# Two pads in SBUF that move every large tile to a multiple of 512 bytes, in a float32 decoder layer on one core

## The chip, the core and the metric

The kernel runs on one NeuronCore of a Trainium2 chip. Its engines are TensorE (PE, with its weight loads shown apart as PEld), VectorE (DVE), ScalarE (ACT), GpSimd (POOL) and SyncE (SP, which here only issues DMAs). The metric is the device time of one execution in microseconds, from outside the program; lower is better.

## What is computed

One layer of a decoder over 1024 positions of width 1024, all in float32. Cut to what matters:

```python
u = rms_norm(h, g_mix);  z = u @ w_in                    # 1024 x 4512 (MLA latents, retention q/k/v/gate, two gates)
q = rms_norm(c_q) @ w_uq;  kv = rms_norm(c_kv) @ w_ukv   # MLA, 8 heads, causal softmax
y_a = causal_block_attention(q_full, k_full, v_a) @ w_proj_mla
y_r = (silu(rg) * head_group_norm(retention_chunkwise(rq, rk, rv))) @ w_proj_ret
h = h + (sigmoid(g_a) * y_a + sigmoid(g_r) * y_r) @ w_out
h = h + cross_attention(rms_norm(h) @ w_xq, rms_norm(mem) @ w_xkv) @ w_xo      # 256 memory rows
up = causal_dwconv(rms_norm(h) @ w_up)                   # 1024 x 5632, three taps
h = h + (silu(up[..., :2816]) * up[..., 2816:]) @ w_down
return rms_norm(h, g_final)
```

## The kernel before

Each float32 product is made of three: both operands are split into a high half, rounded to the type that TensorE multiplies quickly (float32r), and a low half, the difference. `mm3` (line 304) issues them: high weights by high activations (L307), high by low (L312), low weights by high (L313). Every one loads its own 128 x 128 weights and streams up to 512 columns.

The host lays all dense weights out as 168 slabs of 128 x 1024 in the order of use. SP loads a slab of 512 KB into one of the two buffers of `raw`; POOL writes its high half to `wh` (L289) and its low half to `wl` (L291), each with four slots; PE works a slab off in `dense` (line 320): two halves of 512 positions, for each half eight blocks k (or four to six), for each k one `mm3`. The slab's block k is at `wh[:, j, k*128:...]`, so 512 bytes after the one before. The first matmul of a slab that is done frees the slot before it (`w_used`), and POOL goes on. The moving operands are the layer's activations, positions along the columns: `uh`, `ul` (normed input), `yth`, `ytl` (retention's output), `oth`, `otl` (MLA's), `mih`, `mil` (the gated mix), `g0h` to `g1l` (normed for the cross-attention), `xqh`, `xql`, `f0h` to `f1l` (normed for the FFN) and `fah`, `fal` (the FFN's hidden channels, in groups of 6, 6, 6 and 4 blocks).

Not all weights that PE loads are slabs. In the MLA stage `m_pv` (L586) multiplies with the value rows `vrh`, `vrl` as weights, and the probabilities `p1h`, `p1l` (or `p0h`, `p0l`) stream; in the attention over memory the scores have `xqh`, `xql` as weights and `mkh`, `mkl` moving with 256 columns, the values `mvh`, `mvl` as weights and `xph`, `xpl` moving with 512. For the keys and values of the memory (`mth`, `mtl`, 256 columns) the weights are slabs again, and for the MLA queries (384 columns) the slabs `wh`, `wl` move and `cqh`, `cql` are the weights. Transposes go through PE too, with the identity in `cn`.

SBUF is allocated by hand. Long-lived tensors come first, one after the other, through `sb`; all large tiles come from `place(kb, ...)`, which puts tensors `kb` KB above the end of those, over one another in time:

```python
with ExitStack() as st:
    if kb:
        st.enter_context(nc.sbuf_tensor(f"below_{specs[0][0]}", [P, int(kb * 256)], f32))
    return [st.enter_context(nc.sbuf_tensor(n, s, f32r if r else f32)) for n, s, r in specs]
```

Nearly all sizes are multiples of 512 bytes, so the start of the first tensor of `sb`, and of the first of `place`, within 512 bytes is that of all that follow. Before, `raw` starts at byte 16,512 of a partition, `wh` at 24,704 and `wl` at 41,088, ending at 57,472 (128 within 512 bytes for each); the tiles start at 62,784 (320 within 512): `uh`, `hT`, `xqh`, `f1h` and `vrh` there, `f0h`, `xs` and `mih` at 128,320, `fah` at 161,088, `p1h` at 193,856. The identity in `cn` starts at 64 within 512.

Of the kernel before, what the change touches and what calls it, by code (L numbers as in the profile page):

```python
# [26 lines left out]
P = 128  # L27
# [73 lines left out]
def build(nc, x, mem, pos, slabs, small, const, out):  # L101
# [23 lines left out]
    with ctx:  # L125
        def sb(name, shape, dt=f32):
            return ctx.enter_context(nc.sbuf_tensor(name, shape, dt))
# [2 lines left out]
            return ctx.enter_context(nc.semaphore(name))  # L130


        raw = sb("raw", [P, RAWS, 1024])
        wh = sb("wh", [P, SLOTS, 1024], f32r)
        wl = sb("wl", [P, SLOTS, 1024], f32r)
# [9 lines left out]
        rsm = sb("rsm", [P, NT, 2])  # L145
        mst = sb("mst", [P, 3, MB])
        amax, aneg, asum, ainv = (sb(n, [P, 2, CH]) for n in ("amax", "aneg", "asum", "ainv"))
        ps = ctx.enter_context(nc.psum_tensor("ps", [P, 8, H2], f32))


# [1742 lines left out]
```

## Time and profile before

| | |
|---|---|
| timed runs | 2094.06, 2099.07, 2099.65 us; median 2099.07 |
| the profiled execution, first to last instruction | 2093.5 us |
| PE busy | 1955.6 us, 9308 matmuls |
| DVE, ACT, POOL busy | 909.7, 557.9, 850.0 us |
| mean granted clock of TensorE | 0.978 |

The profile shows one execution; of its own time it tells the span alone, which the three timed runs exceed by 0.6, 5.6 and 6.2 us. Busy times say how much of the span an engine works; a group of instructions tells a line, an engine, the tensors written and read, and the shape. A matmul's duration there is from its start to its modelled end, and matmuls overlap. The pace at which PE goes is read from the starts in the timeline: the distance between two rows, divided by the number of matmuls from the one to the other.

### The profile page before, as it was taken

The page shows a single profiled execution, that of the slowest core. Times are in us where ns is not written, and L with a number is a line of the kernel's source. Part 1 is how long each engine was busy: PE and PEld are TensorE (multiplying, and loading weights), DVE is VectorE, ACT ScalarE, POOL GpSimd, SP SyncE. Part 2 cuts the span into 40 slices and gives each one's busy share as a digit, 9 for nine tenths or more (in the row PEclk, how much of TensorE's full clock was granted, in tenths as well). Part 3 has the DMA queues.
Part 4 walks back from the last instruction along what each step waited for, and adds up shares of the span by engine and source line. Part 5 has one row for each costly group of instructions (what it writes and reads, how often), then busy time and mean ns, then how long its engine had stood idle before and what let it go on. Part 6 is the DMA issues. An engine that isn't in the chain of part 4 may idle for free.

```text
span 2093.5 us, 25536 instructions
## 1 busy us (share of the span) xinstructions
PE 1955.6 (93%) x9308; PEld 1595.0 (76%) x9308; DVE 909.7 (43%) x1522; ACT 557.9 (27%) x988; POOL 850.0 (41%) x324
## 2 busy tenths in 40 slices
PE   5999999999978887899998899999999999999987
PEld 4888888888767776677778878787888788878865
DVE  5454540000266665543421633665155415542564
ACT  5222231001245555212223411322022102210223
POOL 5333224565310001244327034445645555455460
PEclk9999999999989999999999999999999999999998
DMA  4101112233100003432114112111111121111111
GB/s 149 41 31 30 40 49 83 89 101 94 41 27 1 1 1 107 159 118 99 42 41 137 35 61 80 41 50 50 61 50 40 54 67 40 50 50 61 50 50 81
DMA packets 35339, 128.39 MB, mean 61 GB/s; under 512 B 4032, under 2 KB 4160, under 8 KB 35264
## 3 DMA queue, kind: packets, MB, share of 16 engines
q1 hardware_dynamic: 25776, 92.72, 14.4%
q10 hardware_dynamic: 9488, 34.61, 4.4%
q8 instruction: 54, 0.88, 0.2%
q14 instruction: 21, 0.17, 0.0%
HBM read 110.54 MB, written 16.78 MB: 61 GB/s over the span
## 4 chain that ended last, share of the span: by engine, by line
PE 76%; DVE 9%; issue 6%; ACT 5%; DMA 2%; POOL 1%; SPq 0%; ACTq 0%; DVEq 0%; POOLq 0%
PE ps L307 23%; PE ps L312 23%; PE ps L313 23%; PE ps L586 3%; POOL wl L282 1%; ACT prow L1014 1%; PE ps L565 1%; ACT pr L1175 1%; DVE p1l L1266 1%; DVE t L1269 1%; DMA xs<-in_x 1%; DVE ul L1269 1%; DVE yb L1773 0%; DVE amax L1539 0%; PE ps L737 0%
## 5 line engine op out<-in xcount | busy, mean ns | idle before, releaser
L289 POOL TENSOR_SCALAR wh<-raw 128x1024 fp32r<-128x1024 f32 x152 | 427.1, 2810 | 1129.5 <-PE ps L307 934.0
L291 POOL TENSOR_TENSOR wl<-raw,wh 128x1024 fp32r<-128x1024 f32 x152 | 384.7, 2531 | 12.7
L307 PE MATMUL ps<-uh,wh 128*128 128x512 f32 (+1 forms) x576 | 230.6, 400 | 2.4 <-DVE ul L1269 2.4
L312 PE MATMUL ps<-ul,wh 128*128 128x512 f32 (+1 forms) x576 | 227.9, 396 | 0.0
L313 PE MATMUL ps<-uh,wl 128*128 128x512 f32 (+1 forms) x576 | 227.9, 396 | 0.0
L307 PE MATMUL ps<-fah,wh 128*128 128x512 f32 x352 | 140.6, 399 | 11.4 <-DVE hF L1611 6.3
L307 PE MATMUL ps<-f0h,wh 128*128 128x512 f32 x352 | 138.9, 395 | 1.3 <-DVE z L1757 1.3
L307 PE MATMUL ps<-f1h,wh 128*128 128x512 f32 x352 | 139.0, 395 | 0.1
L313 PE MATMUL ps<-f1h,wl 128*128 128x512 f32 x352 | 138.8, 394 | 0.0
L312 PE MATMUL ps<-f1l,wh 128*128 128x512 f32 x352 | 138.8, 394 | 0.0
L313 PE MATMUL ps<-f0h,wl 128*128 128x512 f32 x352 | 138.8, 394 | 0.0
L312 PE MATMUL ps<-f0l,wh 128*128 128x512 f32 x352 | 138.8, 394 | 0.0
L313 PE MATMUL ps<-fah,wl 128*128 128x512 f32 x352 | 138.8, 394 | 0.0
L312 PE MATMUL ps<-fal,wh 128*128 128x512 f32 x352 | 138.7, 394 | 0.0
L307 PEld LDWEIGHTS ps<-uh,wh 128*128 128x128 f32 (+1 forms) x576 | 107.5, 187 | 28.4 <-DVE ul L1269 2.6
L313 PEld LDWEIGHTS ps<-uh,wl 128*128 128x128 f32 (+1 forms) x576 | 107.2, 186 | 27.6
L312 PEld LDWEIGHTS ps<-ul,wh 128*128 128x128 f32 (+1 forms) x576 | 107.3, 186 | 25.9
L1221 ACT ACTIVATE ya<-z,sm 128x512 f32<-128x512 f32 x44 | 35.9, 817 | 300.5 <-DVE z L1757 300.5
L1757 DVE TENSOR_TENSOR z<-ps,rbF 128x512 f32<-128x512 f32 x88 | 60.8, 691 | 106.5 <-PE ps L313 103.2
L1791 DVE TENSOR_TENSOR hF<-ps,hF 128x512 f32 x48 | 33.2, 691 | 149.6 <-PE ps L313 149.4
L307 PEld LDWEIGHTS ps<-fah,wh 128*128 128x128 f32 x352 | 65.8, 187 | 34.4 <-issue 9.7
L1269 DVE SCALAR_TENSOR_TENSOR ya<-z,sm,ya 128x512 f32<-128x512 f32 x88 | 67.9, 771 | 53.2 <-ACT ya L1221 49.3
(347 smaller groups left out, 4082.1 us busy)
## 6 DMA issues: line engine op xcount, KB each, us to landing
raw<-in_slabs SPq DMA_DIRECT2D x168, 512.0 KB, 3.6
xs<-in_x SPq DMA_DIRECT2D x8, 512.0 KB, 7.6
s_ga<-sig ACTq DMA_DIRECT2D x8, 512.0 KB, 2.6
s_mr<-mxr ACTq DMA_DIRECT2D x8, 512.0 KB, 4.7
xtile<-in_x ACTq DMA_DIRECT2D x8, 512.0 KB, 6.5
sab<-s_ga ACTq DMA_DIRECT2D x8, 512.0 KB, 4.1
mrb<-s_mr ACTq DMA_DIRECT2D x8, 512.0 KB, 5.1
s_h<-hT ACTq DMA_DIRECT2D x8, 512.0 KB, 2.7
```

Of the source, the lines that this page charges most:

```text
L282: pool.tensor_tensor(wl[:, j, :], raw[:, j % RAWS, :], wh[:, j, :].bitcast(f32), ALU.subtract).then_inc(S["w_ready"], 1)
L289: pool.tensor_scalar(wh[:, j, :], raw[:, j % RAWS, :], 1.0, None, ALU.mult).then_inc(S["w_hi"], 1)
L291: pool.tensor_tensor(wl[:, j, :], raw[:, j % RAWS, :], wh[:, j, :].bitcast(f32), ALU.subtract).then_inc(S["w_ready"], 1)
L307: l = pe.matmul(o, lh, rh, start=start, stop=False)
L312: pe.matmul(o, lh, rl, start=False, stop=False)
L313: return pe.matmul(o, ll, rh, start=False, stop=stop)
L565: l = pe.transpose(ps[:, 6 + q % 2, (c % CH) * P:(c % CH + 1) * P], prow[:, w % 2, c * P:(c + 1) * P], ident)
L586: return pe.matmul(ps[:, 1, qs], vv[:, c, v], pp[:, c, qs], start=start, stop=stop, skip_group_check=True)
L1221: act.activation(y[:, half(b)], z[:, 2 + b * H2:2 + (b + 1) * H2], ACT.Identity, scale=smc("cw2", c + FB * x_), bias=smc("b_conv", c + FB ...
L1269: return dve.scalar_tensor_tensor(out=o, in0=a, scalar=s_, in1=b_, op0=op0, op1=op1)
L1757: dve.tensor_tensor(z[:, 2 + b * H2:2 + (b + 1) * H2], ps[:, b, :], rbF[:, b, :], ALU.mult).then_inc(d_free[b], 1)
L1791: dve.tensor_tensor(hb, ps[:, b, :], hb, ALU.add).then_inc(d_free[b], 1)
```

## The change

Two tensors that nothing reads or writes are allocated: one of 96 float32 (384 bytes per partition) ahead of `raw`, one of 80 (320 bytes) behind the small tensors, ahead of what `place` gives out.

```diff
+        sb("line_up_slabs", [P, 96])
         raw = sb("raw", [P, RAWS, 1024])
         wh = sb("wh", [P, SLOTS, 1024], f32r)
         wl = sb("wl", [P, SLOTS, 1024], f32r)
...
         amax, aneg, asum, ainv = (sb(n, [P, 2, CH]) for n in ("amax", "aneg", "asum", "ainv"))
+        sb("line_up_tiles", [P, 80])
         ps = ctx.enter_context(nc.psum_tensor("ps", [P, 8, H2], f32))
```

The instructions of every engine, their order and their waits are the same ones. Only addresses differ:

| tensors | start within 512 bytes before | after |
|---|---|---|
| `raw`, `wh`, `wl`, `sm` | 128 | 0 |
| `cn` (identity, constants) | 64 | 448 |
| `ones_r`, `ident_r`, `mask_r` | 480 | 352 |
| all first tensors of `place` and what lies behind them in whole 512 bytes (`uh` ... `fal`, `z`) | 320 | 0 |
| `ya`, `yb` (behind `z`, which has 1026 columns) | 352 | 32 |
| `t3`, `t4` | 480 | 160 |
| `zkr`, `krow`, `kr1`, `kr2` | 384 | 64 |

Slabs move up by 384 bytes and tiles by 704. The distance from a slab's start to a tile's, within 512 bytes, is 192 before and 0 after; between two tiles, or two slabs, it is 0 in both.

## Rows read from the trace of the kernel before

**Rows 1.** The page's busy times, and the core's mean granted clock.
```profile
PE 1955.6 (93%) x9308; PEld 1595.0 (76%) x9308; DVE 909.7 (43%) x1522; ACT 557.9 (27%) x988; POOL 850.0 (41%) x324
...
core 0: 2093.5 us, clock 0.978
```

**Rows 2.** The chain that ended last: shares of the span by engine.
```profile
PE 76%; DVE 9%; issue 6%; ACT 5%; DMA 2%; POOL 1%; SPq 0%; ACTq 0%; DVEq 0%; POOLq 0%
```

**Rows 3.** Groups of lines (busy us, mean ns, idle before and its releaser), POOL's split.
```profile
L289 POOL TENSOR_SCALAR wh<-raw 128x1024 fp32r<-128x1024 f32 x152 | 427.1, 2810 | 1129.5 <-PE ps L307 934.0
L291 POOL TENSOR_TENSOR wl<-raw,wh 128x1024 fp32r<-128x1024 f32 x152 | 384.7, 2531 | 12.7
```

**Rows 4.** Groups of lines: wide matmuls with slab weights, L307's of each size.
```profile
L307 PE MATMUL ps<-uh,wh 128*128 128x512 f32 (+1 forms) x576 | 230.6, 400 | 2.4 <-DVE ul L1269 2.4
...
L307 PE MATMUL ps<-f0h,wh 128*128 128x512 f32 x352 | 138.9, 395 | 1.3 <-DVE z L1757 1.3
...
L307 PE MATMUL ps<-mih,wh 128*128 128x512 f32 x128 | 50.8, 397 | 1.1 <-issue 0.9 <-DVE hT L1611 0.2
...
L307 PE MATMUL ps<-g0h,wh 128*128 128x512 f32 x64 | 25.4, 397 | 1.4 <-DVE xf L1656 1.4
```

**Rows 5.** Timeline of PE (start us, duration us), FFN, slab weights, 37 apart.
```profile
1959.78 0.39 PE L313 MATMUL ps<-f1h,wl 128*128 128x512 f32 x1
...
1968.41 0.39 PE L307 MATMUL ps<-f0h,wh 128*128 128x512 f32 x1
```

**Rows 6.** Timeline of PE, MLA's values, weights among the tiles, 3 and 10 apart.
```profile
769.28 0.40 PE L586 MATMUL ps<-p1l,vrh 128*128 128x512 f32 x1
...
769.98 0.39 PE L586 MATMUL ps<-p1h,vrl 128*128 128x512 f32 x1
...
772.24 0.33 PE L586 MATMUL ps<-p1h,vrh 128*128 128x384 f32 x1
```

**Rows 7.** Timeline of PE, values over memory, weights among the tiles, 5 apart.
```profile
1180.67 0.39 PE L307 MATMUL ps<-xph,mvh 128*128 128x512 f32 x1
...
1181.81 0.39 PE L313 MATMUL ps<-xph,mvl 128*128 128x512 f32 x1
```

**Rows 8.** Windows: span, busy us (x) of PE to POOL, granted clock, DMA, GB/s.
```profile
820.00:823.00 3.00, 3.00 (x9) 2.32 (x8) 0.00 (x0) 0.00 (x0) 0.00 (x0) 0.50 0.86 276
...
1700.00:1990.00 290.00, 289.48 (x1239) 231.21 (x1239) 129.72 (x160) 49.92 (x70) 155.71 (x57) 1.00 0.17 52
```

**Rows 9.** Timelines of PE, 256 columns: slab weights, 18 apart; tile weights, 14 apart.
```profile
1105.92 0.28 PE L307 MATMUL ps<-mth,wh 128*128 128x256 f32 x1
...
1107.96 0.28 PE L307 MATMUL ps<-mth,wh 128*128 128x256 f32 x1
...
1190.21 0.28 PE L307 MATMUL ps<-mkh,xqh 128*128 128x256 f32 x1
...
1191.89 0.28 PE L313 MATMUL ps<-mkh,xql 128*128 128x256 f32 x1
```

**Rows 10.** Timeline of PE, MLA's queries, slabs moving with 384 columns, 6 apart.
```profile
574.67 0.34 PE L313 MATMUL ps<-wh,cql 128*128 128x384 f32 x1
...
575.71 0.34 PE L313 MATMUL ps<-wh,cql 128*128 128x384 f32 x1
```

**Rows 11.** Timeline of PE, MLA's values at half the clock, 6 apart.
```profile
820.28 0.63 PE L586 MATMUL ps<-p1h,vrl 128*128 128x512 f32 x1
...
822.84 0.63 PE L586 MATMUL ps<-p1h,vrl 128*128 128x512 f32 x1
```

**Rows 12.** Timelines of POOL and DVE in the last eight slabs.
```profile
2021.21 2.77 POOL L289 TENSOR_SCALAR wh<-raw 128x1024 fp32r<-128x1024 f32 x1 [5.17 <-PE ps L307]
...
2028.39 2.77 POOL L289 TENSOR_SCALAR wh<-raw 128x1024 fp32r<-128x1024 f32 x1 [1.93 <-PE ps L307]
...
2024.39 2.62 DVE L1619 TENSOR_TENSOR acc<-acc,sq 128x512 f32<-128x512 f32 x1 [1.00 <-ACT sq L1082]
```

**Rows 13.** One line of DVE, the convolution's adds: ns min/median/max.
```profile
L1269 DVE SCALAR_TENSOR_TENSOR ya<-z,sm,ya x4: 752/752/752, 1522.0 to 1528.1; 128x512 f32<-128x512 f32 x4
```

## The prediction

> **What bounds the kernel now.** Read first the busy table and the clock of the core: TensorE (PE) is busy for 1955.6 of 2093.5 us, at a mean granted clock of 0.978 [rows 1]. Then the chain of work that ended last: 76% of the span lies on PE, 9% on DVE, 2% on DMA, 1% on POOL [rows 2]. POOL, which splits every weight slab into a high and a low half, needs 2.81 + 2.53 = 5.34 us for one and sat idle for 1129.5 us, of which PE's release of the slot ended 934.0 [rows 3]: it waits for PE, not PE for it. So the kernel's time is, over most of the span, the number of matmuls times the pace at which PE starts them. The mean of a matmul in the groups (0.39 us) is a latency, not that pace; the pace is read from the starts in the timeline of PE.
>
> The wide matmuls are nearly all of one kind: 512 moving columns of an activation tile against 128 columns of a weight slab. In the groups of lines [rows 4] stand 576 of L307 with uh; 352 with f0h (f1h and fah too); 128 with mih (xqh too); 64 with g0h (g1h, yth, oth too). Each has two fellows from L312 and L313. That is 3 x 576 + 9 x 352 + 6 x 128 + 12 x 64 = 6432 matmuls.
>
> **What the change does, part by part.** No instruction is added, removed or moved, on any engine or queue, and no wait either. The two pads are never written or read, so they cost nothing. What is left is where operands start within 512 bytes: slabs from 128 to 0, the large tiles from 320 to 0. The distance between the two, within 512 bytes, goes from 192 to 0. So the whole question is whether an address has a price, and the trace of before holds a comparison for it, since TensorE also multiplies with weights that lie among the tiles.
>
> **The term that matters: PE's pace.** With slab weights (start 128) and a tile (start 320) moving, in the FFN, the first and the last row lie 8.63 us and 37 matmuls apart: 0.2332 us each [rows 5]. With weights in the tile region (vrh, vrl) and p1h, p1l moving, so distance 0, the same 512-wide matmuls in the same order high-high, high-low, low-high go 2.26 us for 10, 0.2260 [rows 6]. Another such place, the attention over memory with mvh, mvl and xph, xpl, shows 1.14 us for 5, 0.228 [rows 7]. With two decimals in the timeline that reads as one step of some 6.7 ns between 0.2333 and 0.2267. Nothing else that I can see sets the two kinds apart: same shapes, same engine, same bank of PSUM for a whole run of matmuls, and the full granted clock, which the FFN has in its row [rows 8] and without which 0.226 is out of reach [rows 11]. The step appears again at 256 columns: 18 matmuls with slab weights take 2.04 us (0.1133), 14 with weights in the tile region take 1.68 us (0.1200) [rows 9]; there the sign is the other one. At 384 columns, with a slab moving and a tile as weights, 6 take 1.04 us, 0.1733 [rows 10]. At half the clock there is no step at all: 0.4267 us each, 6 in 2.56 us, for the pair that at full clock goes 0.226 [rows 8, 11], which is 512 columns at 1.2 GHz and nothing over. So at 2.4 GHz each matmul pays a small toll over its 213.3 ns, between 13 and 20 ns at 512 columns, and this toll comes in steps and depends on the operands.
>
> I choose the distance between the two reads as what it depends on, since that is what differs between [rows 5] and [rows 6, 7], and it fits that all k blocks of a slab (512 bytes apart) go at one pace. After the change every pair has distance 0, so I take 0.2267 for the wide ones: 6.7 ns less. Of the 6432 I leave out two parts. The last eight slabs (192 matmuls) are paced by DVE: POOL's slabs start 7.18 us apart there, where 24 matmuls need only 5.6 us, and DVE's adds for the sum of squares stand between [rows 12]. And some 3%, 190, run at the low clock or just after a wait. 6050 x 6.7 ns = 40.5 us. After a wait the low pace is not there at once: before the ten of [rows 6] three go 0.70 us, 0.233 each. With some 100 waits of PE at 5 matmuls and 5 ns each I take off 2.5 us. The gain is 38 us, all of it on the path where PE is late; if PE becomes quicker, POOL is next, with 5.34 us per slab against 48 x 0.2267 = 10.9 us, or 8.2 us for the slabs with 36 matmuls, so it stays hidden.
>
> **The small terms.** DVE: the two adds of the convolution read z at two starts that are 4 bytes apart, and all last 752 ns [rows 13]; to DVE a start is worth nothing at that distance, and I take 0 for DVE, and for ACT, which streams rows likewise. Even 1% of DVE's 9% of the chain would be 2 us. POOL: hidden. DMA: 4096 bytes per partition go to a start of 128 or 320; on the path they hold 2% of the span [rows 2], some 40 us; I take 0, and with a tenth less or more at either end 4 us each way. The 384 matmuls of 256 columns with slab weights may go from 0.1133 to 0.1200, 2.6 us, if they were on the path; the slabs there wait on POOL's half of the split, 2.53 us against 24 x 0.1133 = 2.7 us, so at most that. The transposes and other narrow matmuls (9308 - 6432 - 384, some 2500) can move by a step either way; for the transposes the distance of the identity to the tile goes from 256 to 64. If a fifth of all the narrow ones move, it is 500 x 6.7 ns = 3.4 us, with either sign. I take 1 us as lost for these together. Sum: 2093.5 - 38 + 1 = 2056.5 us of span. The three timed runs before lie 0.6 to 6.2 us over that span, the median 5.6; carried over, 2062 us.
>
> **What a page would make of it.** The trace has 0.2333 us for a wide matmul where 512 columns at 2.4 GHz are 0.2133. The Trainium skill, "TensorE: Matmul & The Clock Gate", section "Wait — 56ns, not 53.3ns?", gives 215.7 ns from start to start for a warm matmul of that width; it measured bf16, and this is float32. By that figure as the floor the 6050 matmuls could give back 6050 x 17.6 ns = 106 us, which no row here reaches. The skill's "SBUF — State Buffer", section "Who interferes with whom", speaks against the change: TensorE has two read ports, one for the moving operand and one for weights, independent of each other, and waits for nobody. By that rule no start address could matter; [rows 5, 6] speak against a toll that is always the same, but not for what it hangs on.
>
> **The rivals.** (A) The pace hangs on something other than the start within 512 bytes: on the region (slabs lie below byte 57,472 of a partition, vrh and mvh above byte 62,784), or on what else runs. Then all stays as it is. For it: the step is only 3%, and f1h at 62,784 and f0h at 128,320 as moving operands go at one pace in [rows 5]. Against it: [rows 6, 7] are two places with different tiles, and both go at the lower pace. Its time is that of before, 2099 us, give or take 4 for the small terms.
>
> (B) The start counts by itself as well as the distance: all tiles of before, weights and moving alike, start off the 512-byte line, so [rows 6] may still carry one step that goes too. Pace 0.2200, twice the gain: 2062 - 40 = 2022 us. For it: 13 ns of toll are left at distance 0. Against it: the slab as moving operand (128) and the tile (320) carry about the same toll, 12.7 and 13.3 ns [rows 6, 10].
>
> (C) The slower side: distance 0 makes both reads meet and costs a step instead. The mechanism has its place in [rows 9]: at 256 columns, distance 0 goes 0.1200 and distance 192 goes 0.1133. If the wide matmuls with a slab settle at 0.2400, they lose 6050 x 6.7 ns: 2099 + 41 = 2140 us. It decides if the same happens at 512 columns with the slab's starts; from 0.2350 on the kernel would be measurably slower. Against it: [rows 6, 7] are 512 wide at distance 0 and go 0.2260 to 0.2280.
>
> **How the numbers follow.** Forecast 0.54, A 0.22, B 0.12, C 0.12. The predicted time is the forecast's, 2062 us. Forecast and A hold 0.76, so the range must take in B, the nearer one by distance from the forecast: from 2015 (B with 7 us for the small terms) to 2103 (A with 4). C is left out, 0.12. A measurement of this kernel tells some 0.3%, 6 us, from no change. Faster by more than that: forecast and B, 0.66, less 0.01 for a forecast eaten by the small terms, 0.65. Within: A without its tails, 0.20. Slower: C and a tail of A and the forecast, 0.15.
>
> **What would show it.** In the profile of the changed kernel, the timeline of PE in the FFN should have wide matmuls 0.2267 us apart (37 of them in 8.39 us, not 8.63), and the same in the stages with uh, mih and xqh; the stretches of L586 should stay at 0.227 (A, C: no word on it; B: 0.220 there too). PE's busy time should fall by about the same 40 us as the span, DVE, ACT and POOL should keep the mean of each group, and the last eight slabs should still be 7.18 us apart. The forecast is wrong if the FFN's pace is 0.2333 still, or if the pace falls but the span doesn't: then another engine was late after all.

## The result: 35 us less, and the profile after

| | before | changed |
|---|---|---|
| median of the runs | 2099.14 us | 2064.22 us |
| ratio, 95% interval | | 0.9843, 0.9823 to 0.9863 |
| profiled execution, span | 2093.5 us | 2059.1 us |

A second comparison, made later, gave 0.9809 (0.9781 to 0.9838) for the same program (below). The kernel is faster by 1.6 to 1.9%.

The page of the changed kernel (its line numbers are higher by one or two, for the two added lines) has PE busy for 30 us less, with the same 9308 matmuls, and the chain as before; this answers [rows 1, 2]. POOL's split takes as long as it did in [rows 3].

```profile
span 2059.1 us, 25536 instructions
...
PE 1926.0 (94%) x9308; PEld 1605.1 (78%) x9308; DVE 920.7 (45%) x1522; ACT 557.6 (27%) x988; POOL 844.3 (41%) x324
...
PE 76%; DVE 9%; issue 6%; ACT 5%; DMA 2%; POOL 1%; SPq 0%; ACTq 0%; DVEq 0%; POOLq 0%
...
L291 POOL TENSOR_SCALAR wh<-raw 128x1024 fp32r<-128x1024 f32 x152 | 429.9, 2828 | 1105.5 <-PE ps L309 910.0
L293 POOL TENSOR_TENSOR wl<-raw,wh 128x1024 fp32r<-128x1024 f32 x152 | 376.3, 2475 | 12.7
```

The timeline of PE, first in the FFN (rows 37 matmuls apart, to be laid beside [rows 5]), then in the MLA's values with weights among the tiles (10 apart, beside [rows 6]), then at 256 columns with slab weights (18 apart, beside the first two of [rows 9]); the columns are start, duration, engine, line:

```profile
1745.50 0.39 PE L309 MATMUL ps<-f1h,wh 128*128 128x512 f32 x1
...
1753.89 0.39 PE L314 MATMUL ps<-f0l,wh 128*128 128x512 f32 x1
...
739.09 0.39 PE L588 MATMUL ps<-p1h,vrl 128*128 128x512 f32 x1
...
741.36 0.33 PE L588 MATMUL ps<-p1h,vrh 128*128 128x384 f32 x1
...
1090.03 0.28 PE L309 MATMUL ps<-mth,wh 128*128 128x256 f32 x1
...
1092.19 0.28 PE L309 MATMUL ps<-mth,wh 128*128 128x256 f32 x1
```

The FFN goes at 8.39 / 37 = 0.2268 us a matmul, where it was 0.2332. The matmuls whose weights lie among the tiles stay where they were, 2.27 / 10 = 0.227. At 256 columns the slab matmuls became slower, 2.16 / 18 = 0.1200 where it was 0.1133 (over all of them the mean went from 115.2 to 119.8 ns). That is the pattern of distance 0 at both widths.

Where the 34.4 us of the two spans went, stage by stage, is read from the first start of the first matmul on each tile (worked out from the timelines; the third column is the second profile of the same program):

| stage | before | changed | changed, second profile |
|---|---|---|---|
| to the first matmul with uh | 36.5 | 36.2 | 35.6 |
| retention and first gates (uh) | 356.1 | 353.7 | 349.1 |
| second gates and latents (yth on) | 174.9 | 172.3 | 169.5 |
| MLA, its queries and softmax | 260.7 | 258.4 | 262.9 |
| mix and output (xtile, oth, mih) | 157.5 | 154.2 | 153.8 |
| query projection (g0h) | 102.8 | 102.1 | 100.5 |
| memory and attention over it | 128.7 | 128.1 | 129.3 |
| its output (xqh) | 89.7 | 87.2 | 88.8 |
| FFN up to the last eight slabs | 702.8 | 687.2 | 685.7 |
| last eight slabs | 56.2 | 52.1 | 50.9 |
| to the end | 27.6 | 27.7 | 27.5 |

### The profile page after: what moved, and what is told of

The parts are those of the page before. It is cut to its first block, busy times and chain, and to the rows that moved or that the text cites. A ratio compares the mean times of both kernels' runs of the same rounds, so it can differ in the third digit from the quotient of the medians.

```text
span 2059.1 us, 25536 instructions
## 1 busy us (share of the span) xinstructions
PE 1926.0 (94%) x9308; PEld 1605.1 (78%) x9308; DVE 920.7 (45%) x1522; ACT 557.6 (27%) x988; POOL 844.3 (41%) x324
## 4 chain that ended last, share of the span: by engine, by line
PE 76%; DVE 9%; issue 6%; ACT 5%; DMA 2%; POOL 1%; SPq 0%; ACTq 0%; DVEq 0%; POOLq 0%
PE ps L309 23%; PE ps L314 23%; PE ps L315 23%; PE ps L588 3%; POOL wl L284 1%; ACT prow L1016 1%; PE ps L567 1%; ACT pr L1177 1%; DVE p1l L1268 1%; DVE t L1271 1%; DVE amax L1541 1%; DMA xs<-in_x 1%; DVE ul L1271 1%; DVE yb L1775 1%; PE ps L383 0%
## 5 line engine op out<-in xcount | busy, mean ns | idle before, releaser
L293 POOL TENSOR_TENSOR wl<-raw,wh 128x1024 fp32r<-128x1024 f32 x152 | 376.3, 2475 | 12.7
L309 PE MATMUL ps<-uh,wh 128*128 128x512 f32 (+1 forms) x576 | 229.3, 398 | 3.3 <-DVE ul L1271 3.3
L1271 DVE SCALAR_TENSOR_TENSOR ya<-z,sm,ya 128x512 f32<-128x512 f32 x88 | 86.2, 979 | 53.2 <-ACT ya L1223 49.3
L1457 DVE TENSOR_TENSOR mxr<-ps,sig 128x512 f32<-128x512 f32 x16 | 11.1, 692 | 177.9 <-PE ps L315 177.9
```

Source lines behind the costliest of these rows:

```text
L293: pool.tensor_tensor(wl[:, j, :], raw[:, j % RAWS, :], wh[:, j, :].bitcast(f32), ALU.subtract).then_inc(S["w_ready"], 1)
L309: l = pe.matmul(o, lh, rh, start=start, stop=False)
L1271: return dve.scalar_tensor_tensor(out=o, in0=a, scalar=s_, in1=b_, op0=op0, op1=op1)
```

## The experiments

All of them leave the instructions and their order as they are and change only where tensors start. "Distance" is a tile's start less a slab's, within 256 or 512 bytes; wherever a kernel's rows of PE are shown, they are 37 wide matmuls apart, in the FFN unless another place is named.

**One pad each.** The first kernel has the pad ahead of the slabs alone, the second the one ahead of the tiles alone:

```diff
         sb("line_up_slabs", [P, 96])
...
-        sb("line_up_tiles", [P, 80])
```

> Only the pad ahead of the slabs (384 bytes). Slabs then start at 0 within 512 bytes, tiles at 192: the distance is 192, as before the change, with both starts others than before. Theory 1 (the toll of a matmul hangs on the distance between where weights and moving operand start, within 512 bytes): wide matmuls with slab weights stay at 0.2333 us, the 256-wide ones at 0.1133, about 2095 to 2100 us. Theory 2 (what counts is that an operand itself starts at a multiple of 512; the slabs do now): half of the gain or more, a pace of 0.2300 or less, 2080 us or less. Theory 3 (the region above some byte counts, and any shift would have done it): 0.2267, about 2064 us.

```diff
-        sb("line_up_slabs", [P, 96])
...
         sb("line_up_tiles", [P, 80])
```

> Only the pad ahead of the tiles (320 bytes). Slabs start at 128 within 512 bytes as before, tiles at 128 too: distance 0, but nothing starts at a multiple of 512. Theory 1 (distance): the whole gain, pace 0.2267 us, 0.1200 at 256 columns, about 2064 us. Theory 2 (multiples of 512): no gain, 0.2333, about 2099 us.

The first came to 2095.17 us against 2097.11 before on the same chip, ratio 0.9999 (0.9980 to 1.0018); the second to 2058.33, ratio 0.9823 (0.9794 to 0.9852). First pad alone, then second pad alone:

```profile
1764.16 0.39 PE L314 MATMUL ps<-f0h,wl 128*128 128x512 f32 x1
...
1772.79 0.39 PE L308 MATMUL ps<-f1h,wh 128*128 128x512 f32 x1
```

```profile
1745.48 0.39 PE L313 MATMUL ps<-f1l,wh 128*128 128x512 f32 x1
...
1753.86 0.39 PE L314 MATMUL ps<-f0h,wl 128*128 128x512 f32 x1
```

8.63 us and 8.38 us for 37: 0.2332 and 0.2265 us. With slabs at a multiple of 512 bytes and tiles at 192, nothing is gained; with both at 128, where nothing lies at a multiple, everything is. This settles between the theories: multiples of 512 bytes are worth nothing in themselves, and neither is a shift as such. What counts is where the two operands of a matmul start relative to each other. The second kernel also rules out the region: its slabs lie where they lay before.

**Which distances.** A tile pad of (320 + d) / 4 float32 instead of 80 puts the tiles d bytes further, with the slabs at 0:

```diff
-        sb("line_up_tiles", [P, 80])
+        sb("line_up_tiles", [P, 96])      # d = 64; 144 for 256, 112 for 128, 88 for 32, 136 for 224
```

> Both pads, the second 64 bytes longer: slabs at 0, tiles at 64, distance 64. Theory 1 (distance within 512 bytes): a pace of its own, in steps of 6.7 ns from 0.2200 to 0.2400 us, the same for all wide matmuls with slab weights; matmuls with weights among the tiles (distance still 0) stay at 0.2267. Theory 2 (multiples of 512): both kinds leave 0.2267, for 0.2333 or more, since no tile starts at a multiple.

> Both pads, the second 256 bytes longer: slabs at 0, tiles at 256, distance 256. If the pattern of theory 1 (distance) repeats every 256 bytes, it is as after: 0.2267 us at 512 columns and 0.1200 at 256, about 2064 us. If it repeats only every 512, a pace of its own between 0.2200 and 0.2400. Theory 2 (multiples of 512): 0.2333 or more for both kinds of weights.

> Slabs at 0, tiles at 128: distance 128. So far 0 and 256 gave 0.2267 us, 64 gave 0.2289 and 192 gave 0.2333, at 512 columns with slab weights. If the toll grows steadily from 0 to 192 and falls back at 256: about 0.2311, some 2080 us. If it depends on whether the distance is a multiple of 128: 0.2267, some 2058 us.

> Slabs at 0, tiles at 32: distance 32. If only lines of 64 bytes count, the pace is that of distance 0, 0.2267 us, and the span some 2057 us. If the distance counts to the byte, a pace between those of 0 and 64, about 0.2278, some 2060 us.

> Slabs at 0, tiles at 224: distance 224, or 32 short of the next repeat. Steady growth to 192 and a fall to 256 puts it at 0.2300 to 0.2333 us, 2075 to 2095 us; if there is a distance with less toll than 0, it could be here, at 0.2200, some 2020 us, since a start just short of the slab's has not been tried.

Distance 64, then 256:

```profile
1745.99 0.39 PE L315 MATMUL ps<-f1h,wl 128*128 128x512 f32 x1
...
1754.46 0.39 PE L309 MATMUL ps<-f0h,wh 128*128 128x512 f32 x1
```

```profile
1745.42 0.39 PE L309 MATMUL ps<-f1h,wh 128*128 128x512 f32 x1
...
1753.80 0.39 PE L314 MATMUL ps<-f1l,wh 128*128 128x512 f32 x1
```

Distance 128, then 32, then 224:

```profile
1762.64 0.40 PE L315 MATMUL ps<-f0h,wl 128*128 128x512 f32 x1
...
1771.25 0.39 PE L309 MATMUL ps<-f1h,wh 128*128 128x512 f32 x1
```

```profile
1769.33 0.40 PE L315 MATMUL ps<-f0h,wl 128*128 128x512 f32 x1
...
1777.96 0.39 PE L309 MATMUL ps<-f1h,wh 128*128 128x512 f32 x1
```

```profile
1764.35 0.40 PE L315 MATMUL ps<-f0h,wl 128*128 128x512 f32 x1
...
1772.99 0.40 PE L309 MATMUL ps<-f1h,wh 128*128 128x512 f32 x1
```

8.47, 8.38, 8.61, 8.63 and 8.64 us for 37. Distance 256 is distance 0 again, at both widths, so I take the pattern to repeat every 256 bytes (0 and 256 are the only such pair tried); and since 64 and 192 differ (0.2289 here, 0.2333 before the change), it does not repeat every 128. It isn't a steady rise from 0 either: 32 costs as much as 192, and 64 costs a third of it.

**Sixteen bytes off.** Both weight tensors are made 256 bytes larger and used from an offset, in the kernel before, without pads:

```diff
-        wh = sb("wh", [P, SLOTS, 1024], f32r)
+        wh = sb("wh", [P, SLOTS * 1024 + 64], f32r)[:, 52:52 + SLOTS * 1024].rearrange("p (s n) -> p s n", s=SLOTS)
```

and the same for `wl`; the offset is 52 for distance 240 and 44 for 16.

> Slabs start 16 bytes behind the tiles within 256 bytes (both views moved inside their tensors, no pads ahead): distance 240. The nearest distances measured, 224 and 0, gave 0.2333 and 0.2267 us. Theory 1, only exact alignment within 256 bytes helps: 0.2333 or close to it, some 2090 us. Theory 1c, what counts is the distance in lines of 32 bytes or more: 0.2267, some 2058 us. A distance with less toll than 0 would show as 0.2200, some 2020 us.

> As the last, with slabs 16 bytes ahead of the tiles within 256 bytes: distance 16, between 0 (0.2267 us) and 32 (0.2333). Theory 1: 0.2333 or close to it, some 2095 us. Theory 1c (coarser lines): 0.2267, some 2058 us. Less toll than at 0: 0.2200, some 2020 us.

Distance 240, then 16:

```profile
1767.00 0.39 PE L313 MATMUL ps<-f0h,wl 128*128 128x512 f32 x1
...
1775.63 0.40 PE L307 MATMUL ps<-f1h,wh 128*128 128x512 f32 x1
```

```profile
1745.89 0.39 PE L313 MATMUL ps<-f0h,wl 128*128 128x512 f32 x1
...
1754.34 0.39 PE L307 MATMUL ps<-f0h,wh 128*128 128x512 f32 x1
```

8.63 and 8.45 us. A slab that starts 16 bytes later than the tile, within 256, loses the whole gain in the FFN; one that starts 16 bytes earlier loses a fifth of it on average. Neither is better than 0, and 0.2200 was seen nowhere.

But these two kernels also show that the distance does not fix the pace alone. Rows 37 apart in the query projection at distance 240, then in an earlier stretch of the FFN at distance 16:

```profile
1038.26 0.39 PE L307 MATMUL ps<-g0h,wh 128*128 128x512 f32 x1
...
1046.64 0.39 PE L312 MATMUL ps<-g1l,wh 128*128 128x512 f32 x1
```

```profile
1389.73 0.39 PE L307 MATMUL ps<-f0h,wh 128*128 128x512 f32 x1
...
1398.12 0.39 PE L312 MATMUL ps<-f1l,wh 128*128 128x512 f32 x1
```

8.38 and 8.39 us, the pace of distance 0. At distance 16 the FFN goes at 226.7 ns from 1312 to 1436 us and at 228.3 from 1445 us on, with the same tensors `f0h` to `f1l` at the same addresses in both. At distance 240 the matmuls with g0h to g1l from 1005 us on go at 226.7 and those of the FFN at 233.3. So at these distances PE can go at either of two paces for a hundred microseconds, and what sets which one is not shown.

In one table, with the mean over all FFN matmuls with slab weights (some 3120 steps between starts, those after a wait left out) and the time of the program:

| distance | starts, slab / tile | ns per matmul, FFN | us |
|---|---|---|---|
| 0 | 0 / 0 (changed) | 226.7 | 2064.2, 2056.0 |
| 0 | 128 / 128 | 226.7 | 2058.3 |
| 256 | 0 / 256 | 226.7 | 2057.5, 2056.8 |
| 16 | 48 / 64 within 256 | 228.1 (226.7 in one stretch) | 2064.5 |
| 32 | 0 / 32 | 233.3 | 2101.4 |
| 64 | 0 / 64 | 228.9 | 2064.1 |
| 128 | 0 / 128 | 232.4 | 2088.8 |
| 192 | 128 / 320 (before) | 233.3 | 2099.1 |
| 192 | 0 / 192 | 233.3 | 2095.2 |
| 224 | 0 / 224 | 233.3 | 2091.3 |
| 240 | 80 / 64 within 256 | 233.3 | 2098.8 |

Runs of one program scatter by some 5 us, so the times of the rows with a single run order only roughly; the paces of two profiles with one distance agree within 0.1 ns, and through all of these kernels the 256-column matmuls with both operands among the tiles stayed at 119.6 to 119.8 ns on average. Between stages the mean differs little (227.4 ns outside the FFN at distance 0, where some steps follow waits), except at distance 240, with 231.9 outside the FFN, and at 16, where the stage with mih went at 226.8, the pace of distance 0.

**Only the low halves off.** A pad of 64 bytes between the high and the low slabs puts the tiles at distance 0 from `wh` and 192 from `wl`:

```diff
         wh = sb("wh", [P, SLOTS, 1024], f32r)
+        sb("line_up_low", [P, 16])
         wl = sb("wl", [P, SLOTS, 1024], f32r)
...
-        sb("line_up_tiles", [P, 80])
+        sb("line_up_tiles", [P, 64])
```

> As the changed kernel, but the low halves of the slabs (wl) start at 64 instead of 0: the tiles are at distance 0 from the high halves (wh) and at 192 (256 - 64) from the low ones. The three matmuls of a product, L307, L312, L313 before, have weights wh, wh, wl; while L312 streams, the weights wl of L313 are loaded. Theory 1a (the toll comes from the weight load that runs at the same time as the moving operand is read): the start of L313 comes 0.2333 us after that of L312, the other two steps are 0.2267, on average 0.2289. Theory 1b (it is the matmul's own weights and moving operand whose distance counts): the step after L313, to the next L307, is the long one. Both give about 2070 us; without such a theory of pairs the pace would be 0.2267 or 0.2333 for all three.

```profile
1759.57 0.40 PE L316 MATMUL ps<-f0h,wl 128*128 128x512 f32 x1
...
1768.13 0.39 PE L310 MATMUL ps<-f1h,wh 128*128 128x512 f32 x1
```

8.56 us, 0.2314; the mean over the FFN is 231.1 ns, and its time 2088.4 us (2095.1 before, on the same chip). From the starts of the three lines, the step after the high-high matmul is 228.5 ns, after high-low 229.3 and after low-high (L316, with `wl` as its own weights) 235.7. The long step follows the matmul whose own operands are at distance 192 and not the one that streams while `wl` is loaded, as theory 1b has it. But theory 1b gave 228.9 on average, and 231.1 was measured: one pair in three off costs two thirds of the gain. And at distance 64, where all three pairs are alike, the steps are unequal too (226, 229, 232, in stretches that put the long one behind different lines). So the pair matters, yet its steps don't simply add up, and whether it is a matmul's own weights or what the loads before left behind is not shown.

**The changed kernel again, beside distance 256.**

> The changed kernel once more, beside the next one on the same chip: about 2064 us, PE's pace 0.2267 us. In its profile before, DVE's adds of the convolution's first half (ya) took 979 ns on average instead of 771, sixteen of them over 1 us, since they met POOL's split. If that is a matter of this kernel's timing it shows again here; if it was one execution's, the group is back at 771.

> Distance 256 with slabs at 0, timed. By theory 1 with a repeat of 256 bytes it is the changed kernel in all that counts, so the same time within 0.3%. If the 16 slow adds of DVE belong to the changed kernel and cost time, it is 3 to 6 us faster than that one; if multiples of 512 bytes have some worth of their own, it is slower.

2055.96 us, ratio 0.9809 (0.9781 to 0.9838), and 2056.75 us, ratio 0.9804 (0.9777 to 0.9831), against 2096.45 before. The two are one in time. The second profile of the changed kernel has the same pace:

```profile
1745.51 0.39 PE L315 MATMUL ps<-f0h,wl 128*128 128x512 f32 x1
...
1753.89 0.39 PE L309 MATMUL ps<-f1h,wh 128*128 128x512 f32 x1
```

and DVE's adds are back. The group of lines in the first profile of the changed kernel, then in the second:

```profile
L1271 DVE SCALAR_TENSOR_TENSOR ya<-z,sm,ya 128x512 f32<-128x512 f32 x88 | 86.2, 979 | 53.2 <-ACT ya L1223 49.3 <-DVE ya L1271 0.8
```

```profile
L1271 DVE SCALAR_TENSOR_TENSOR ya<-z,sm,ya 128x512 f32<-128x512 f32 x88 | 67.9, 772 | 53.2 <-ACT ya L1223 49.3 <-DVE ya L1271 0.8
```

The 979 ns were that one execution's, not the change's; distance 16's profile has this group at 893 ns, one of the two of distance 256 at 801, and all the others at 771 or 772, so DVE and POOL seem to meet there in single executions now and then.

## Why the prediction was right

**The pace and what sets it.** The term that carried the sum was a step of 6.7 ns for the wide matmuls, read off the trace of before by comparing places where weights and moving operand lie at distance 192 with places where they lie at 0. It measured 233.3 - 226.7 = 6.6 ns in the FFN, and 6.5 or 6.6 with mih and xqh; with uh, the largest group outside the FFN, it was 5.6 on average (233.2 to 227.6), since about a tenth of these steps, in stretches, still took 230 to 236 ns. The choice of distance as the cause, with 0.54, was right: the second pad alone does the whole work, the first alone nothing. The FFN up to its last slabs shows it most plainly: 15.6 us less, 17.1 in the second profile, where its 3168 - 192 = 2976 matmuls times 6.6 ns could give 19.6. The rest is idle time of PE, which in this stage grew from 3.3 to 6.2 us (4.0 in the second profile), and a short fall to the half clock as the FFN begins, 1.7 us in both profiles, which the one of before does not have. PE's busy time fell by 29.6 us, and 34.7 in the second profile, where 40 were forecast.

**The repeat was put too wide.** I worked within 512 bytes; 256 fits all that was tried. This cost nothing here, since 0 is 0 in both. That the toll "comes in steps" of 6.7 ns does not hold: 228.3, 228.9 and 232.4 ns lie between, and at distances 16 and 240 one distance has two paces.

**The 256-column matmuls.** Forecast at 0.1200, measured at 0.1200, from a mean of 115.2 ns rather than 113.3; 384 x 4.6 ns is 1.8 us at most, within the 2.6 that the prediction allowed, and it can't be told from the rest: the stage of the memory went from 128.7 to 128.1 us, and to 129.3 in the second profile. This is rival C's mechanism, present but only at that width.

**The last eight slabs: the step that failed.** I left them out, as paced by DVE, and wrote that they would still be 7.18 us apart. POOL's split and DVE's adds for the sum of squares in the changed kernel, beside [rows 12]:

```profile
1999.66 2.77 POOL L291 TENSOR_SCALAR wh<-raw 128x1024 fp32r<-128x1024 f32 x1 [2.12 <-PE ps L309]
...
2005.10 3.00 POOL L291 TENSOR_SCALAR wh<-raw 128x1024 fp32r<-128x1024 f32 x1 [0.18 <-PE ps L309]
...
2009.37 1.78 DVE L1621 TENSOR_TENSOR acc<-acc,sq 128x512 f32<-128x512 f32 x1 [1.01 <-ACT sq L1084]
```

The slabs are 5.44 us apart, which is 24 matmuls at 0.2267, so PE sets the pace there (at distances 128 and 224 they are 5.57 and 5.60 apart, again 24 times PE's pace), and POOL, with 5.4 us of work for a slab, has next to no idle time left. DVE's adds, which before took 1.35 or 2.62 us in turn (four slabs long), now take 0.69 us, but for three of 1.63 to 1.78. What paced this stretch was not DVE's own work but the way its adds met POOL's split in a pattern that kept itself going: before, too, once POOL has split its last slab (at 2048.0 us), every add takes 0.69 us and PE's slabs are 5.7 and 5.6 us apart. By the groups of lines, the adds' mean fell from 940 ns to 785 to 790 at distances 0, 16, 64 and 256, but also at 128 (785) and 224 (786), where PE's pace in the FFN is nearly or wholly the old one; it stayed at 940 with the first pad alone, at 32, at 240 and with only the low halves off. So a quicker pace isn't needed to break the pattern.

What decides it can be read where DVE's first add of these slabs meets the split, before and changed:

```profile
2020.57 0.47 PE L307 MATMUL ps<-fah,wh 128*128 128x512 f32 x1 [1.30 <-DVE hF L1611]
...
2021.43 1.36 DVE L1619 TENSOR_TENSOR acc<-acc,sq 128x512 f32<-128x512 f32 x1 [1.00 <-ACT sq L1082]
```

```profile
1990.91 0.77 PE L309 MATMUL ps<-fah,wh 128*128 128x512 f32 x1 [1.08 <-DVE hF L1613]
...
1991.76 0.69 DVE L1621 TENSOR_TENSOR acc<-acc,sq 128x512 f32<-128x512 f32 x1 [1.00 <-ACT sq L1084]
...
1991.84 3.24 POOL L291 TENSOR_SCALAR wh<-raw 128x1024 fp32r<-128x1024 f32 x1 [6.14 <-PE ps L309]
```

The PE row is the second slab's first matmul, which frees a slot and so releases POOL's split. The add starts 0.86 us after it in both. Before, the matmul takes 0.47 us, the split starts first (at 2021.21, [rows 12]), and the add, 0.22 us behind, takes 1.36. In the changed kernel the matmul takes 0.77 us, for TensorE had just fallen to the half clock, as eleven us around this point show (the column after the counts is the granted clock):

```profile
2016.00:2027.00 11.00, 7.86 (x30) 5.32 (x30) 8.06 (x9) 3.12 (x5) 5.21 (x3) 1.00 0.16 48
```

```profile
1986.00:1997.00 11.00, 9.02 (x21) 6.62 (x22) 5.61 (x9) 3.12 (x5) 5.08 (x2) 0.53 0.15 48
```

So the split starts 0.07 us behind the add instead of ahead of it; the add takes 0.69 us, and the split 3.24 in place of 2.77. This sorts all fourteen profiles. In the nine without the pattern (both of the changed kernel, the second pad alone, both of distance 256, and 16, 64, 128, 224) that matmul runs at the half clock, 0.76 or 0.77 us, and the add comes 0.07 us ahead of the split. In the five with it (before, the first pad alone, 32, 240, only the low halves off) it runs at the full clock, 0.47 us, and the split comes 0.22 us ahead. No run sets the clock by itself, and why it falls there in some is not shown; all five profiles with distance 0 or 256 have the fall, neither of the two with 192 has it.

The times of 128 and 224, one run each, 2088.8 and 2091.3 us beside 2095.1 before on the same chip, don't speak against a gain where the pattern is gone, but lie within the scatter. In the changed kernel the stretch is 4.1 us shorter, 5.3 in the second profile, the slow matmuls included, where I had put nothing.

**What was lost elsewhere.** The stages with uh gave 2.4 + 2.6 us in the first profile where their 1920 matmuls should have given 12.7; in the second they gave 7.0 + 5.4. The difference is mostly the clock. Both stages together, from the first matmul with uh to the first on `cqh`, before, changed, and changed in the second profile:

```profile
36.50:567.50 531.00, 522.25 (x2541) 427.15 (x2541) 149.08 (x344) 100.94 (x159) 222.34 (x86) 0.99 0.19 59
```

```profile
36.20:562.30 526.10, 516.88 (x2541) 430.78 (x2541) 149.02 (x344) 100.78 (x158) 222.09 (x86) 0.98 0.19 60
```

```profile
35.60:554.10 518.50, 509.33 (x2541) 425.30 (x2541) 148.97 (x344) 100.47 (x158) 222.08 (x86) 1.00 0.19 61
```

PE does the same 2541 matmuls and is idle for 9 us in all three. Half of the time at the half clock, worked out from the trace, is 4.5 us before, 9.9 in the first profile and 1.7 in the second. Less that, the two stages gained 10.4 and 9.6 us, near the 12.7; 1.7 of what is missing is the smaller step with uh. Such falls of the clock come and go between executions, and belong to the few us by which runs of one program differ.

So the sum of 37 us of span was made of one term of the right size, one that was missing (4 to 5 us) and an allowance for the low clock and the waits that ran a little short; the two comparisons gave 35 and 40 us. That the forecast of 2062 us met 2064.2 so closely is in part luck: the missing term and the losses nearly cancelled there, and in the second comparison, with 2056.0 us, they did not.

**The rivals.** A (the region or the neighbours count) falls with the second pad alone, which left the slabs in their region and gave the whole gain, and with the first pad alone, which moved the slabs and everything above them for nothing. B (a start's own alignment gives a second step) falls with L588's pace, 0.227 with tiles at 0 as with tiles at 320, and with the second pad alone. C was not to be seen at 512 columns; that distance 0 is best there is not trivial, since of the distances tried (256 counts as 0) only 16 and 64 keep most of the gain. By the Trainium skill, "SBUF — State Buffer", section "Who interferes with whom", where TensorE's two read ports are independent and it waits for nobody, no address should have had an effect; the runs show one of 3% at the full clock, and the measurement decides. The 215.7 ns that the skill's "TensorE: Matmul & The Clock Gate" gives for bf16 (section "Wait — 56ns, not 53.3ns?") were reached at no distance with float32.

## What to carry to other kernels

Where TensorE is the bound, read its pace from the starts in the timeline and divide, for every kind of operand that the kernel has; if one kind goes quicker at the same shape, look at where its operands start. For float32 (float32r) matmuls of 512 columns it paid to let weights and moving operand start at the same place within 256 bytes; a pad of a few hundred bytes does it. At 256 columns the same distance was the slowest one (119.8 ns against 115), so count which width the kernel has more of. And where two engines collide in a fixed pattern, don't take its period as given: here 0.3 us more in one matmul, which ran at the half clock, turned the order of the two and made the pattern go, in seven of eleven other placements.

## What the runs showed of the hardware that I had not expected

- The start-to-start time of 512-column float32r matmuls at the full clock depends on the distance of weights and moving operand within 256 bytes, from 226.7 ns (0, also for other absolute starts) to 233.3 (32, 192, 224, 240), with 228.1 at 16, 228.9 at 64 and 232.4 at 128; these are means over the FFN. At 256 columns the order is another one: 119.8 ns at 0, 114.8 to 115.2 at 192, 116.9 at 32, 117.5 at 64. At half the clock there is nothing of it: matmuls with slab weights are 426 or 427 ns apart at every distance tried, as those of [rows 11].
- 16 bytes count, and not alike in both directions (228.1 and 233.3 in the FFN). At these two distances PE can also go at 226.7 ns for long stretches, with the same tensors.
- A lock between DVE's adds and POOL's split holds or falls with which of them starts first, by 0.22 us one way or 0.07 the other, and that with TensorE's clock at one matmul.
- Four bytes do nothing on DVE [rows 13], where adds with starts 4 bytes apart take the same 752 ns.
- The cause inside the chip stays open. A conflict of the two reads in banks that repeat every 256 bytes would fit the repeat, but not plainly the value at 32, nor that one pair in three costs two thirds, nor the two paces at 16 and at 240; it was only argued.
